# First two weight panels abreast and loaded in halves, a zeroed tile on TensorE before them, and other planner costs in the first block

## The chip, the cores and the metric

The kernel runs on one core of a Trainium2 chip. TensorE (PE; its weight loads are shown as PEld) multiplies, VectorE (DVE), ScalarE (ACT) and GpSimd (POOL) do the elementwise work, and SyncE (SP) issues all DMAs from one queue in order. The metric is the device time of one execution in microseconds; the profiled execution is one of them, looked at by the hardware profiler.

## The reference

Two transformer blocks follow one another on x of 512 tokens by 1024 features, all in float32. Of the first block the part that matters here is its beginning:

```
h = rmsnorm(x) * norm_mix_g
z = h @ w_in                      # 1024 x 5888: qa, ka, va, qb, kb, vb, ga, gb
y_a = mixer_a(qa, ka, va)         # 8 heads of full attention, 2 key/value heads, axial rope
y_b = mixer_b(qb, kb, vb)         # 3 groups of 4 heads, dilated bands, relative bias by bucket
x = x + (sigmoid(ga + b) * (y_a @ w_out_a) + sigmoid(gb + b) * (y_b @ w_out_b)) @ w_out
x = x + relu(rmsnorm(x) @ w_ff1)**2 @ w_ff2
x = x + sigmoid(rmsnorm(x) @ w_ple_gate) * (p @ w_ple)
```

A final norm and the second block follow: a SwiGLU layer, a mixer of retention and differential attention, attention to a memory, a second SwiGLU layer and the output norm.

## The kernel before, in words

Activations lie transposed, features on the 128 partitions and the 512 tokens along the row, so x is 8 tiles of 128x512 (256 KB each). Every float32 operand is split into a high part and a low part in a faster format, and a product is three matmuls: high by high, high weight by low activation, low weight by high activation. The weights come as panels: a panel is 8 blocks of 128x128 side by side (128x1024, 512 KB), it gives one 128x512 output tile, and it takes 8 x 3 = 24 matmuls, one triple per x tile. `take` (L456) makes a panel: one load from the packed weights, two ScalarE copies (`p.th`, tile `wh`, L467) that make the high part in halves of 512 columns, and two VectorE or four GpSimd subtractions (`p.tl`, tile `wl`, L469) that make the low part. Raw, high and low each have three buffers, so a panel's load waits for the low part of the panel three before.

Nothing is ordered by the hardware alone: `build` writes one list per engine, and each engine runs its list strictly in order, with semaphore waits. The lists come from a planner. Each helper (`v_tt`, `a_act`, `b_mm`, ...) appends an operation and moves the engine's planned clock by a cost formula; DMAs get a planned landing time from `dma_fin`. `flow` holds jobs (generators: a normalisation, a head's scores, a softmax, a split) and fills (panels). It steps the first job whose input is planned to be ready 0.15 us before TensorE's planned clock, and otherwise puts one more triple of a panel on TensorE. So the cost formulas decide after how many panel matmuls each step of a job is written into the lists, and `sooner` chooses VectorE or GpSimd by them.

A panel's parts are placed by `place_panels` at marks that the panels before it leave: the load on SP at the end of the panel five before (panels 0 to 4 at marks written out by hand, `first_load`), high and low parts one per step of the panel two before (panel 2's after the last step of panel 0, panels 0 and 1 after the rows of x tiles 0 and 3).

The beginning: SP loads the gain columns, x tile 0, panel 0, x tiles 1 to 4, panel 1, x tiles 5 to 7, a table `mats`, panel 2, three small tables (`relb`, `hot`, `mask`), panels 3 and 4, then `sel` and `rope` (about 0.5 MB each). `first_rows` makes h's high part (ScalarE) and low part (VectorE) of each x tile; `first_sum` squares the 8 tiles on ScalarE and adds them on VectorE for the norm's scale. `relative` makes the relative-bias table: three full-precision matmuls of `hot` and `relb`, an addition of `mask` on VectorE, a store to DRAM (`d_tab`, eight copies of each row), and twelve gathers from it into the bias tiles, which wait for the store. The panels come in the order qb, kb of group 0, 1 and 2 (panels 0 to 5), then vb, and so on. A head group's scores (`scores_b`) need the two projected tiles split, and two of the four PSUM banks that jobs use; those are released by VectorE's addition of the bias (tile `pB`).

Of the kernel before, what the change touches and what calls it, by code (L numbers as in the profile page):

```python
# [5 lines left out]
KT = DM // 128  # L6
# [18 lines left out]
NHOT = NX0 + 2 * NX1  # L25

# [66 lines left out]
def build(nc, d):  # L93
# [80 lines left out]
    def a_act(out, in_, func, *waits, **kw):  # L174
        cost = 0.1 + 0.00082 * size(in_) + 0.06 * ("bias" in kw) + 0.08 * ("accum_out" in kw)
        if "scale" in kw and not isinstance(kw["scale"], float):
            cost += 0.1
        return act.add(lambda e: e.activation(out, in_, func, **kw), cost, waits)  # L178

    def v_tt(out, a, b, op, *waits):  # L180
        return dve.add(lambda e: e.tensor_tensor(out, a, b, op), 0.065 + 0.00105 * size(a), waits)  # L181

    def v_stt(out, a, s, b, op0, op1, *waits, rev=False):
        return dve.add(lambda e: e.scalar_tensor_tensor(out, a, s, b, op0, op1, reverse0=rev), 0.1 + 0.00105 * size(a), waits)  # L184

    def v_ts(out, a, s1, s2, op0, op1, *waits):
        return dve.add(lambda e: e.tensor_scalar(out, a, s1, s2, op0, op1), 0.12 + 0.0006 * size(a), waits)

    def v_red(out, a, op, *waits, negate=False):
        return dve.add(lambda e: e.tensor_reduce(out, a, X, op, negate=negate), 0.065 + 0.00105 * size(a), waits)  # L190

    def v_cp(out, a, *waits):
        return dve.add(lambda e: e.tensor_copy(out, a), 0.065 + 0.00105 * size(a), waits)

    def v_ttr(out, a, b, scale, first, op0, op1, acc, *waits):
        return dve.add(lambda e: e.tensor_tensor_reduce(out, a, b, scale, first, op0, op1, acc), 0.08 + 0.00105 * size(a), waits)

    def v_rcp(out, a, *waits):
        return dve.add(lambda e: e.reciprocal(out, a), 0.07 + 0.0063 * size(a), waits)

    def p_tt(out, a, b, op, *waits):
        return pool.add(lambda e: e.tensor_tensor(out, a, b, op), 0.1 + 0.0022 * size(a), waits)  # L202
# [4 lines left out]
    def p_mul(out, a, s, *waits):  # L207
        return pool.add(lambda e: e.tensor_scalar(out, a, s, 1.0, ALU.mult, ALU.mult), 0.07 + 0.0012 * size(a), waits)
# [6 lines left out]
    def e_tt(out, a, b, op, *waits):  # L215
        n = size(a)
        return (v_tt if sooner(waits, 0.065 + 0.00105 * n, 0.2 + 0.0022 * n) else p_tt)(out, a, b, op, *waits)

    def e_mul(out, a, s, *waits):
        n = size(a)  # L220
        return (v_mul if sooner(waits, 0.12 + 0.0006 * n, 0.17 + 0.0012 * n) else p_mul)(out, a, s, *waits)

    table = [None]
# [64 lines left out]
    def b_mm(bank, out, lhsT, rhs, *waits):  # L288
        first, w = opened(bank)
        n = 0.0025 + size(rhs) / 2400  # L290
        n = max(n, 0.055) if lhsT.dtype == F32R else max(4 * n, 0.108)
        bank.done = pe.add(lambda e: e.matmul(out, lhsT, rhs, start=first, stop=True, skip_group_check=True), n, w, waits)  # L292
        return bank.done
# [143 lines left out]
    first_loads, first_parts = [], []  # L437
# [8 lines left out]
    def parts_here(after):  # L446

        low = (dve if not first_parts else pool) if len(panels) < 3 else panels[-1].low
        act.t = max(act.t, after) + 1.04
        low.t = max(low.t, act.t - 0.5) + (2.4 if low is pool else 1.2)  # L450

    def take(s):

        p = Panel()
        p.i, p.n = len(panels), len(s[3])
        i, width = p.i, s[2] * p.n  # L456
        p.width, p.off = width, panels[-1].off + 128 * panels[-1].width if panels else 0
        panels.append(p)
        order.append(s)
        src = d["wts"][p.off:p.off + 128 * width].rearrange("(p n) -> p n", p=128)  # L460
        raw, p.H, p.L = raw_t[i % 3], wh_t[i % 3], wl_t[i % 3]
        H, L = p.H, p.L
        behind = max(dve.t, pe.t) + 1.2 > max(pool.t, pe.t) + 2.4
        p.low = low = pool if (behind if i > 3 else i > 0) else dve
        p.cut = 256 if low is pool else 512
        p.load = Op(sp, lambda e: e.dma_start(raw[:, 0:width], src), [panels[i - 3].tl] if i >= 3 else [], raw_sem[i % 3])
        p.th = [Op(act, lambda e, c=c: e.activation(H[:, c], raw[:, c], FN.Copy), [p.load])  # L467
                for c in (slice(o, min(o + 512, width)) for o in range(0, width, 512))]
        p.tl = [Op(low, lambda e, c=c: e.tensor_tensor(L[:, c], raw[:, c], H[:, c].bitcast(F32), ALU.subtract),  # L469
                   [p.load, p.th[c.start // 512]]) for c in (slice(o, min(o + p.cut, width)) for o in range(0, width, p.cut))]  # L470
# [12 lines left out]
    def ran(p):  # L483

        p.steps.append(marks())
        if len(p.steps) == 3:
            parts_here(panels[p.i - 1].done.fin if p.i else 0.0)

    def place_panels():
        for p in panels:  # L490
            if p.i >= 3:
                assert panels[p.i - 3].done is not None
                p.th[0].waits.append(panels[p.i - 3].done)
            if p.i >= 5:
                panels[p.i - 5].steps[-1][sp].append(p.load)
            else:
                first_loads[p.i].append(p.load)
            for n, op in enumerate(p.th + p.tl):
                if p.i >= 2:
                    at_ = panels[p.i - 2].steps  # L500
                    at_[min(1 + n, len(at_) - 1) if p.i > 2 else -1][op.lane].append(op)
                else:
                    first_parts[p.i][op.lane].append(op)
# [18 lines left out]
    def panel(s, ops, ring, then, n=512, leave=None):  # L522
# [5 lines left out]
        spawn(then(b))  # L528

# [316 lines left out]
    def first_rows(k):  # L846
# [3 lines left out]
        if k in (0, 3):  # L850
# [25 lines left out]
    first_load()  # L876
    first_load()
# [11 lines left out]
    def relative():  # L889
# [10 lines left out]
        t_row = dma(tab_d, tab_t[:, :].unsqueeze(1).to_broadcast([4, COPIES, NHOT]), s_row, [tk for _, tk in parts])  # L900
        for g, wd in enumerate((256, 128, 128)):
# [16 lines left out]
    def proj_b(pr, g, i):  # L918
# [17 lines left out]
        return panel(feat("w_in", (QB, KB_)[i] + 128 * (2 * g + pr)), h1, FIL, then)  # L936
# [456 lines left out]
    for pr in range(2):  # L1393
        for g in range(3):
            for i in range(2):
                fills.append(proj_b(pr, g, i))
# [229 lines left out]

    RQ, RK, RV, RG, DQ, DK, DV = (512 * i for i in range(7))
    r, rcol = Rstd(21), Rstd()
    e = now()
# [793 lines left out]
```

How the kernel before makes its waits and increments, by code:

```python
            def go(eng):  # L2358
                for op in queues[ln]:
                    for key, value in op.emit:
                        eng.wait_ge(key.sem, value)
                    ins = op.fn(eng)
                    if isinstance(op.sem, DmaSem):
                        ins.then_inc(op.sem.sem, 16)
                    elif op.used:
                        ins.then_inc(ln.sem, 1)
                if ln is sp:
                    for o in outs:
                        eng.wait_ge(o.sem.sem, o.value)
```

## Time and profile before

| what | us |
|---|---|
| median of three runs (2056.57 to 2057.57) | 2057.19 |
| profiled execution | 2057.28 |
| its span, first to last instruction | 2055.4 |
| TensorE busy (9854 matmul records) | 2023.5 |
| VectorE / ScalarE / GpSimd busy | 1123.9 / 889.6 / 344.4 |
| mean granted TensorE clock | 0.995 |

Start times are counted from the span's first instruction. A row of the timeline gives the start, the duration, the engine, the line, the operation, what it writes and reads, how many were merged, and in brackets how long the engine was idle before and what ended that. A busy TensorE is not TensorE at its peak, since records of neighbouring matmuls overlap and a matmul at half clock is busy for longer. A granted clock of 1.00 is the 2.4 GHz level, 0.50 the 1.2 GHz level.

### The profile page before, as it was taken

The page shows a single profiled execution, that of the slowest core. Times are in us where ns is not written, and L with a number is a line of the kernel's source. Part 1 is how long each engine was busy: PE and PEld are TensorE (multiplying, and loading weights), DVE is VectorE, ACT ScalarE, POOL GpSimd, SP SyncE. Part 2 cuts the span into 40 slices and gives each one's busy share as a digit, 9 for nine tenths or more (in the row PEclk, how much of TensorE's full clock was granted, in tenths as well). Part 3 has the DMA queues.
Part 4 walks back from the last instruction along what each step waited for, and adds up shares of the span by engine and source line. Part 5 has one row for each costly group of instructions (what it writes and reads, how often), then busy time and mean ns, then how long its engine had stood idle before and what let it go on. Part 6 is the DMA issues. An engine that isn't in the chain of part 4 may idle for free.

```text
span 2055.4 us, 25244 instructions
## 1 busy us (share of the span) xinstructions
PE 2023.5 (98%) x9854; PEld 1684.2 (82%) x9854; DVE 1123.9 (55%) x1964; ACT 889.6 (43%) x1750; POOL 344.4 (17%) x337
## 2 busy tenths in 40 slices
PE   8999999999999999999999999999999999999997
PEld 6888778888888888878888888788898888888886
DVE  6767774455434344665443435787775664443434
ACT  5545553345423233553232325777655453322224
POOL 3224330021000001432110101232211021110102
PEclk9999999999999999999999999999999999999999
DMA  5221112243232322233323223223342033233322
GB/s 186 83 73 62 42 43 74 78 158 111 94 101 92 103 92 88 89 103 102 100 94 103 92 82 116 74 73 103 102 140 83 28 116 102 92 95 101 97 87 72
DMA packets 61635, 191.53 MB, mean 93 GB/s; under 512 B 6792, under 2 KB 14472, under 8 KB 61516
## 3 DMA queue, kind: packets, MB, share of 16 engines
q1 hardware_dynamic: 61516, 189.93, 28.7%
q8 instruction: 77, 1.26, 0.2%
q14 instruction: 42, 0.34, 0.1%
HBM read 187.69 MB, written 2.21 MB: 92 GB/s over the span
## 4 chain that ended last, share of the span: by engine, by line
PE 92%; DVE 5%; ACT 1%; DMA 1%; issue 1%; SPq 0%; DVEq 0%; ACTq 0%
PE bank L292 90%; PE bank L297 1%; DVE wl L469 1%; DVE work L190 1%; DVE tmp L181 0%; SPq L169 0%; ACT wh L467 0%; DMA raw<-d_wts 0%; DMA d_tab<-tab_sb 0%; ACT pB L178 0%; ACT rsq L178 0%; DVE x_sb L181 0%; DVE tmp L184 0%; DVE work L181 0%; DVE ssum L181 0%
## 5 line engine op out<-in xcount | busy, mean ns | idle before, releaser
L467 ACT ACTIVATE wh<-raw 128x512 fp32r<-128x512 f32 (+1 forms) x700 | 403.7, 610 | 891.4 <-PE bank L292 887.6
L292 PE MATMUL bank<-h_h,wh 128*128 128x512 f32 x1536 | 609.9, 397 | 7.3 <-ACT wh L467 6.1
L292 PE MATMUL bank<-h_l,wh 128*128 128x512 f32 x1536 | 600.6, 391 | 1.3 <-DVE h_l L184 1.2
L292 PE MATMUL bank<-h_h,wl 128*128 128x512 f32 x1536 | 600.1, 391 | 0.0
L469 DVE TENSOR_TENSOR wl<-raw,wh 128x512 fp32r<-128x512 f32 (+1 forms) x632 | 423.1, 695 | 60.9 <-ACT wh L467 38.8
L292 PEld LDWEIGHTS bank<-h_h,wh 128*128 128x128 f32 x1536 | 289.6, 189 | 71.1 <-ACT wh L467 6.1
L292 PEld LDWEIGHTS bank<-h_l,wh 128*128 128x128 f32 x1536 | 289.8, 189 | 63.5 <-DVE h_l L184 3.7
L292 PEld LDWEIGHTS bank<-h_h,wl 128*128 128x128 f32 x1536 | 289.5, 188 | 61.0 <-DVE wl L469 0.3
L469 POOL TENSOR_TENSOR wl<-raw,wh 128x256 fp32r<-128x256 f32 x134 | 107.1, 826 | 350.5 <-ACT wh L467 350.5
L202 POOL TENSOR_TENSOR tmp<-tmp,rstd 128x512 f32<-128x512 f32 x44 | 63.4, 1442 | 469.4 <-ACT tmp L178 469.4
L181 DVE TENSOR_TENSOR tmp<-bank,rstd 128x512 f32<-128x512 f32 x98 | 70.4, 721 | 115.1 <-PE bank L292 114.5
L181 DVE TENSOR_TENSOR x_sb<-x_sb,bank 128x512 f32<-128x512 f32 x56 | 38.5, 687 | 141.2 <-PE bank L292 141.2
L181 DVE TENSOR_TENSOR tmp<-tmp,bank 128x512 f32<-128x512 f32 x53 | 36.4, 687 | 139.3 <-PE bank L292 133.1
L184 DVE SCALAR_TENSOR_TENSOR x_sb<-bank,x_sb 128x512 f32<-128x512 f32 (+1 forms) x51 | 33.6, 660 | 123.5 <-PE bank L292 123.5
L292 PE MATMUL bank<-f1act_h,wh 128*128 128x512 f32 x256 | 99.6, 389 | 0.0
L292 PE MATMUL bank<-f1act_l,wh 128*128 128x512 f32 x256 | 99.6, 389 | 0.0
L292 PE MATMUL bank<-f1act_h,wl 128*128 128x512 f32 x256 | 99.6, 389 | 0.0
L202 POOL TENSOR_TENSOR ssum<-ssum,tmp 128x512 f32<-128x512 f32 (+1 forms) x52 | 70.6, 1362 | 134.4 <-ACT tmp L178 133.3
L202 POOL TENSOR_TENSOR ssum<-tmp,tmp 128x512 f32<-128x512 f32 (+1 forms) x9 | 12.4, 1385 | 472.9 <-ACT tmp L178 472.9
L292 PE MATMUL bank<-f3act_h,wh 128*128 128x512 f32 (+1 forms) x194 | 71.8, 370 | 0.0
L292 PE MATMUL bank<-f3act_h,wl 128*128 128x512 f32 (+1 forms) x194 | 71.7, 369 | 0.0
L292 PE MATMUL bank<-f3act_l,wh 128*128 128x512 f32 (+1 forms) x194 | 71.6, 369 | 0.0
(476 smaller groups left out, 3317.0 us busy)
## 6 DMA issues: line engine op xcount, KB each, us to landing
raw<-d_wts SPq DMA_DIRECT2D x314, 512.0 KB, 3.5
raw<-d_wts SPq DMA_DIRECT2D x24, 384.0 KB, 3.0
x_sb<-d_xT SPq DMA_DIRECT2D x16, 256.0 KB, 5.5
raw<-d_wts SPq DMA_DIRECT2D x24, 128.0 KB, 2.0
d_yT<-x_sb SPq DMA_DIRECT2D x4, 384.0 KB, 2.9
tab<-d_ali SPq DMA_DIRECT2D x4, 256.0 KB, 4.3
tab<-d_dec SPq DMA_DIRECT2D x4, 256.0 KB, 3.8
mraw<-d_memT SPq DMA_DIRECT2D x8, 128.0 KB, 2.4
```

The source lines that it names most:

```text
L181: return dve.add(lambda e: e.tensor_tensor(out, a, b, op), 0.065 + 0.00105 * size(a), waits)
L184: return dve.add(lambda e: e.scalar_tensor_tensor(out, a, s, b, op0, op1, reverse0=rev), 0.1 + 0.00105 * size(a), waits)
L190: return dve.add(lambda e: e.tensor_reduce(out, a, X, op, negate=negate), 0.065 + 0.00105 * size(a), waits)
L202: return pool.add(lambda e: e.tensor_tensor(out, a, b, op), 0.1 + 0.0022 * size(a), waits)
L292: bank.done = pe.add(lambda e: e.matmul(out, lhsT, rhs, start=first, stop=True, skip_group_check=True), n, w, waits)
L297: bank.done = pe.add(lambda e: e.transpose(out, in_, ident), 0.11, w, waits)
L467: p.th = [Op(act, lambda e, c=c: e.activation(H[:, c], raw[:, c], FN.Copy), [p.load]) for c in (slice(o, min(o + 512, width)) for o in ran ...
L469: p.tl = [Op(low, lambda e, c=c: e.tensor_tensor(L[:, c], raw[:, c], H[:, c].bitcast(F32), ALU.subtract), [p.load, p.th[c.start // 512]]) ...
```

## The change

It has five parts. At the start VectorE zeroes a 128x128 piece of a scratch tile and TensorE multiplies it by itself nine times in full precision; ScalarE's table for exponentials is loaded there too. The columns go behind x tile 0, and panels 0 and 1 are loaded in halves of 512 columns, in turn with x tiles 1 to 3; both get their low parts on VectorE, one half after each of the rows 0 to 3. Panels 0 and 1 run abreast: for each x tile three matmuls of the one, then three of the other. Panel 5's load moves ahead of `sel` and `rope`, the job `relative` yields between its store and the gathers (so the gathers are written when the planner's clock has passed the store's landing), and panels 2 and 3 have their parts placed at other steps. Until the second block's mixer (`late`) the planner uses other, mostly larger costs, and `ran` books the cost of a panel's parts step by step.

```
+    zero = T.slots[-1].ap[:, 0:128]
+    t_zero = dve.add(lambda e: e.memset(zero, 0.0), 0.2)
+    b = ALL.get()
+    for _ in range(WARM):                                  # WARM = 9
+        b_mm(b, b.ap[:, 0:128], zero, zero, t_zero)
+    b.free = [b.done]
+    T.slots[-1].free = [b.done]
+    act_table(EXP)
+    load_x([0])
     t_cols = dma(cols_t[:, :], d["cols"], DmaSem("s_cols"))
-    def first_load():
+    def first_load(kb=512):
         first_loads.append(sp.mark())
-        return dma_fin(512 * 1024, 0.0)
-    load_x([0])
-    w_fin = [first_load()]
-    load_x([1, 2, 3, 4])
-    w_fin.append(first_load())
-    load_x([5, 6, 7])
+        return dma_fin(kb * 1024, 0.0)
+    w_fin = []
+    for k in range(4):
+        if k:
+            load_x([k])
+        w_fin.append(first_load(256))
+    load_x([4, 5, 6, 7])
...
-        if k in (0, 3):
+        if k < 4:
             parts_here(w_fin[len(first_parts)])
             first_parts.append(marks())
...
-    first_load()
-    first_load()
+    for _ in range(3):
+        first_load()
     t_sel = dma(sel_t[:, :], d["sel"], DmaSem("s_sel"))
...
         t_row = dma(tab_d, tab_t[:, :].unsqueeze(1).to_broadcast([4, COPIES, NHOT]), s_row, [tk for _, tk in parts])
+        yield [t_row]
...
+        if i < 2:
+            p.loads = [Op(sp, lambda e, c=c: e.dma_start(raw[:, c], src[:, c]), [], raw_sem[i] if c.start else DmaSem(f"s_raw{i}a"))
+                       for c in (slice(0, 512), slice(512, width))]
...
-            if p.i >= 5:
-                panels[p.i - 5].steps[-1][sp].append(p.load)
+            if p.i >= 6:
+                panels[p.i - 5].steps[-1][sp].extend(p.loads)
...
-                    at_[min(1 + n, len(at_) - 1) if p.i > 2 else -1][op.lane].append(op)
+                    at_[min(n + (1 if p.i > 3 else 7 if p.i == 2 else KT), len(at_) - 1)][op.lane].append(op)
...
+    def abreast(items, ops, ring):
+        if not ring.idle(len(items))():
+            yield ring.idle(len(items))
+        bs, ps = [ring.get() for _ in items], [take(s) for s, _ in items]
+        for k, t in enumerate(ops):
+            if t.rdy is None:
+                yield have(t)
+            for b, p in zip(bs, ps):
+                ...
+                b_mm(b, out, wH, t.h, high(p, k), t.rdy[0])
+                b_mm(b, out, wH, t.l, t.rdy[1])
+                p.done = b_mm(b, out, wL, t.h, low(p, k))
+                ran(p)
+                yield
```

The costs, in us for a row of n elements (left before, right until `late` is set):

```
ScalarE  activation       0.1   + 0.00082 n     0.19 + 0.00085 n   (accumulator +0.08 / +0.19)
VectorE  tensor_tensor    0.065 + 0.00105 n     0.14 + 0.00108 n
VectorE  scalar_tensor_t. 0.1   + 0.00105 n     0.16 + 0.00108 n
VectorE  tensor_scalar    0.12  + 0.0006 n      0.22 + 0.00053 n
GpSimd   tensor_tensor    0.1   + 0.0022 n      0.15 + 0.00235 n
TensorE  split formats    max(0.0025 + n/2400, 0.055)     max(0.013 + n/2400, 0.111 or 0.06)
```

## Rows read from the trace of the kernel before

**Rows 1.** Table by stretch: busy us (instructions) per engine, granted clock, DMA share, GB/s.
```profile
0.00:6.14 6.14, 0.00 (x1) 0.00 (x1) 0.75 (x1) 2.69 (x4) 0.20 (x4) 1.00 0.61 194
6.14:18.31 12.17, 11.11 (x30) 6.51 (x30) 9.23 (x12) 10.15 (x19) 3.72 (x4) 1.00 0.92 319
24.12:58.83 34.71, 32.85 (x178) 26.43 (x176) 22.62 (x44) 19.86 (x53) 11.22 (x15) 1.00 0.39 126
...
200.00:320.00 120.00, 112.45 (x537) 91.55 (x537) 90.16 (x176) 63.46 (x143) 43.21 (x45) 0.96 0.13 42
320.00:880.00 560.00, 560.00 (x2480) 463.79 (x2479) 265.17 (x404) 218.18 (x376) 57.39 (x53) 1.00 0.31 100
```

**Rows 2.** List of waits, TensorE, 200 to 330 us: total, times, longest.
```profile
PE bank L297 <- DVE pa L187: 3.7, 1, 3.7
```

**Rows 3.** Timeline of TensorE, first 25 us.
```profile
6.14 0.79 PE L292 MATMUL bank<-h_h,wh 128*128 128x512 f32 x1 [6.14 <-ACT wh L467]
...
18.31 1.67 PE L292 MATMUL bank<-hot_sb,relb_sb 32*4 32x383 f32 x6
...
24.12 0.39 PE L292 MATMUL bank<-rsqr,m1024r 128*128 128x512 f32 x1
```

**Rows 4.** DMA view, 0 to 60 us in 40 slices of 1.5 us.
```profile
GB/s 0 106 360 300 332 412 396 414 416 266 133 156 410 413 77 0 85 284 33 35 0 116 147 130 154 137 245 401 391 38 0 0 0 0 191 377 134 8 0 0
```

**Rows 5.** Timeline of VectorE and ScalarE, 13 to 21 us.
```profile
13.03 3.19 DVE L184 SCALAR_TENSOR_TENSOR h_l<-x_sb,cols_sb,h_h 128x512 fp32r<-128x512 f32 x3 [1.59 <-ACT h_h L178]
14.43 0.31 ACT L178 ACTIVATE m1024r<-mats_sb 128x128 fp32r<-128x128 f32 x1 [0.28 <-DMA mats_sb<-d_mats]
14.65 4.26 ACT L178 ACTIVATE tmp<-x_sb 128x512 f32<-128x512 f32 x8
18.82 2.18 ACT L467 ACTIVATE wh<-raw 128x512 fp32r<-128x512 f32 x4
```

**Rows 6.** Timeline of SP's DMA issues, 16 to 38 us.
```profile
16.09 0.43 SPq L169 DMA_DIRECT2D sel_sb<-d_sel  x1
16.56 0.43 SPq L169 DMA_DIRECT2D rope_sb<-d_rope  x1
23.62 0.33 SPq L466 DMA_DIRECT2D raw<-d_wts  x1
23.99 0.77 SPq L169 DMA_DIRECT2D d_tab<-tab_sb  x1
30.48 7.30 SPq L169 DMA_DIRECT2D bias<-d_tab  x12
```

**Rows 7.** Chain of waits in order of time: start, us, what.
```profile
23.99 6.47 DMA d_tab<-tab_sb
```

**Rows 8.** Timeline of VectorE at the first bias additions.
```profile
40.46 0.69 DVE L181 TENSOR_TENSOR pB<-bank,bias 128x512 f32<-128x512 f32 x1 [3.96 <-DMA bias<-d_tab]
41.79 0.68 DVE L181 TENSOR_TENSOR pB<-bank,bias 128x512 f32<-128x512 f32 x1
```

**Rows 9.** Timeline of TensorE: first scores' first and last row, second scores' two waits.
```profile
35.55 0.39 PE L292 MATMUL bank<-qb001h,qb000h 64*128 64x256 f32 x2
...
37.08 0.28 PE L292 MATMUL bank<-qb001l,qb000h 64*128 64x192 f32 x2
47.69 0.33 PE L292 MATMUL bank<-qb011h,qb010h 64*128 64x128 f32 x2 [0.59 <-ACT qb011h L178]
48.76 0.33 PE L292 MATMUL bank<-qb011l,qb010h 64*128 64x128 f32 x2 [0.63 <-DVE qb011l L181]
```

**Rows 10.** Table by stretch, TensorE alone: busy us (records), granted clock, DMA share, GB/s.
```profile
220.03:223.44 3.41, 3.41 (x11) 0.50 0.07 26
281.47:284.88 3.41, 2.28 (x16) 1.00 0.51 156
284.88:291.70 6.82, 5.40 (x15) 0.50 0.00 0
```

**Rows 11.** Groups of instructions on VectorE, 0 to 320 us: busy us, mean ns.
```profile
L181 DVE TENSOR_TENSOR tmp<-bank,rstd 128x512 f32<-128x512 f32 x22 | 18.3, 830 | 2.8 <-PE bank L292 2.8
```

More of the change, by code:

```diff
@@ L192, in v_cp @@
     def v_cp(out, a, *waits):
[L193 removed]
+        return dve.add(lambda e: e.tensor_copy(out, a), (0.065 + 0.00105 * size(a) if late else 0.14 + 0.00108 * size(a)), waits)
     def v_ttr(out, a, b, scale, first, op0, op1, acc, *waits):
[L196 removed]
+        return dve.add(lambda e: e.tensor_tensor_reduce(out, a, b, scale, first, op0, op1, acc), (0.08 + 0.00105 * size(a) if late else 0.22 + 0.00108 * size(a)), waits)
@@ L207, in p_mul @@
     def p_mul(out, a, s, *waits):
-        return pool.add(lambda e: e.tensor_scalar(out, a, s, 1.0, ALU.mult, ALU.mult), 0.07 + 0.0012 * size(a), waits)
+        return pool.add(lambda e: e.tensor_scalar(out, a, s, 1.0, ALU.mult, ALU.mult), (0.07 + 0.0012 * size(a) if late else 0.17 + 0.0016 * size(a)), waits)
     def sooner(waits, dve_cost, pool_cost):
@@ L446, in parts_here @@
     def parts_here(after):
-        low = (dve if not first_parts else pool) if len(panels) < 3 else panels[-1].low
-        act.t = max(act.t, after) + 1.04
-        low.t = max(low.t, act.t - 0.5) + (2.4 if low is pool else 1.2)
+        act.t = max(act.t, after) + 0.61
+        dve.t = max(dve.t, act.t) + 0.69
     def take(s):
@@ L462, in take @@
         H, L = p.H, p.L
-        behind = max(dve.t, pe.t) + 1.2 > max(pool.t, pe.t) + 2.4
-        p.low = low = pool if (behind if i > 3 else i > 0) else dve
+        if late and i not in lows:
+            lows[i] = pool if max(dve.t, pe.t) + 1.2 > max(pool.t, pe.t) + 2.4 else dve
+        p.low = low = lows.pop(i) if i in lows else pool if i > 1 else dve
         p.cut = 256 if low is pool else 512
-        p.load = Op(sp, lambda e: e.dma_start(raw[:, 0:width], src), [panels[i - 3].tl] if i >= 3 else [], raw_sem[i % 3])
-        p.th = [Op(act, lambda e, c=c: e.activation(H[:, c], raw[:, c], FN.Copy), [p.load])
+        if i < 2:
+            p.loads = [Op(sp, lambda e, c=c: e.dma_start(raw[:, c], src[:, c]), [], raw_sem[i] if c.start else DmaSem(f"s_raw{i}a"))
+                       for c in (slice(0, 512), slice(512, width))]
+        else:
+            p.loads = [Op(sp, lambda e: e.dma_start(raw[:, 0:width], src), [panels[i - 3].tl] if i >= 3 else [], raw_sem[i % 3])]
+        p.th = [Op(act, lambda e, c=c: e.activation(H[:, c], raw[:, c], FN.Copy), [p.loads[c.start // 512 if i < 2 else 0]])
                 for c in (slice(o, min(o + 512, width)) for o in range(0, width, 512))]
         p.tl = [Op(low, lambda e, c=c: e.tensor_tensor(L[:, c], raw[:, c], H[:, c].bitcast(F32), ALU.subtract),
-                   [p.load, p.th[c.start // 512]]) for c in (slice(o, min(o + p.cut, width)) for o in range(0, width, p.cut))]
+                   [p.th[c.start // 512].waits[0], p.th[c.start // 512]])
+                for c in (slice(o, min(o + p.cut, width)) for o in range(0, width, p.cut))]
         p.done, p.steps = None, [marks()]
@@ L485, in ran @@
         p.steps.append(marks())
-        if len(p.steps) == 3:
-            parts_here(panels[p.i - 1].done.fin if p.i else 0.0)
+        if late and len(p.steps) == 3:
+            act.t = max(act.t, panels[p.i - 1].done.fin) + 1.04
+            panels[-1].low.t = max(panels[-1].low.t, act.t - 0.5) + (2.4 if panels[-1].low is pool else 1.2)
+        if late:
+            return
+        n, i = len(p.steps) - 2, p.i + 2
+        if n == 0 and not late:
+            behind = max(dve.t, pe.t) + 1.39 > max(pool.t, pe.t) + 3.2
+            lows[i] = pool if (behind if i > 3 else i > 1) else dve
+        if n < 2:
+            act.t = max(act.t, panels[p.i - 1].done.fin + 0.13 if p.i else 0.0) + 0.61
+            th_fin[i, n] = act.t
+        elif i in lows or panels[-1].i >= i:
+            low = lows[i] if i in lows else panels[i].low
+            if low is dve and n < 4:
+                dve.t = max(dve.t, th_fin[i, n - 2] + 0.13) + 0.69
+            elif low is pool and n < 6:
+                pool.t = max(pool.t, th_fin[i, (n - 2) // 2] + 0.13) + 0.8
     def place_panels():
@@ L935, in then @@
             t.free = yield from split(qk[pr][g][i], t.ap[:, :], tk)
-        return panel(feat("w_in", (QB, KB_)[i] + 128 * (2 * g + pr)), h1, FIL, then)
+        return feat("w_in", (QB, KB_)[i] + 128 * (2 * g + pr)), then
     def proj_vb(g, pr):
@@ L1394, in build @@
         for g in range(3):
-            for i in range(2):
-                fills.append(proj_b(pr, g, i))
+            both = [proj_b(pr, g, i) for i in range(2)]
+            if pr == g == 0:
+                fills.append(abreast(both, h1, FIL))
+            else:
+                fills.extend(panel(s, h1, FIL, then) for s, then in both)
         fills.extend(proj_vb(g, pr) for g in (1, 2, 0))
@@ L1623, in build @@
     sm = sm_next[0]
+    late.append(True)
     RQ, RK, RV, RG, DQ, DK, DV = (512 * i for i in range(7))
```

45 lines of the change are left out of this document (30 added, 15 removed).

## The prediction

> **What bounds the kernel now.** I read the table of stages first, because the share of busy time (98% on TensorE) is an average over very different stretches. From 320 to 880 us TensorE is busy all 560 us at a granted clock of 1.00: the change reorders work there at most, and there is nothing to win [rows 1]. What the first block loses lies in four places of the same table: 6.14 us before the first matmul, then 12.17 us that hold only 30 records, 1.86 us idle between 24 and 59 us, and 7.55 us idle between 200 and 320 us, where the mean clock is 0.96. The list of waits gives the largest single piece of the last: 3.7 us for a normalised softmax block on VectorE [rows 2]. Then I followed the chain of waits from the other end. Up to 59 us it does not run over TensorE but over the relative-bias table: the table's store to DRAM takes 6.47 us [rows 7], the twelve gathers are then issued one by one until 37.78 [rows 6], and VectorE waits for the last until 40.46 [rows 8]. So the start of this kernel has two limits side by side, the loads of x and the bias table, and a gain on one counts only as far as the other lets it.
>
> **The start (half loads, two panels abreast, zeroed tile).** Today the first matmul waits for panel 0's high part, which waits for all of its 512 KB; 30 matmuls are done at 18.31, then the bias table's own matmuls take 1.67, and the other 18 of the first two panels end at 24.12: (24.12 - 19.98) / 18 = 0.23 us each [rows 3]. In the new queue x tile 0, the columns and half a panel are ahead of the first matmul, 256 KB less; at the 300 to 416 GB/s of the first slices [rows 4] that is 0.6 to 0.9 us, so it starts at about 5.4. What stands ahead of the last x tile is the same 3 MB in both orders. Its low part ends today at 13.03 + 3.19 = 16.22 [rows 5]; the new order puts panel 1's two low parts on VectorE between the tiles (some 1.4 us more) and takes GpSimd's four away from beside them, and I leave it at 16.3. With two panels abreast each tile feeds 6 matmuls instead of 3, so 5 tiles, again 30 matmuls, can be done at about 15.4.
>
> Then comes a point that the diff does not touch. The planner emits the bias-table matmuls when its TensorE clock has passed the due time of the three small tables (13.6 us by its own DMA sum, with the same bytes ahead as before). By its new sums TensorE passes that after tile 4 of both panels: after the 30th matmul, as today. On the chip mats land at 14.43 [rows 5]; 512 KB of panel 2 and 127 KB of tables follow, 639 KB at 0.4 MB per us = 1.6, an estimate of 16.0; at 18.31 they were there, as no wait for them is shown. Between the two I take 16.4, near the estimate. Then 16.4 + 1.7 + 18 x 0.23 = 22.2, against 24.12: 1.9 us won. Bounds: 2.9 with the tables already there (15.4 instead of 16.4), 0 if they land at 18.3. The memset, the nine zero matmuls and the early table load lie before any x tile is there and cost nothing; if the zero tile ended late, it would push the first matmul by as much, at most 1 us.
>
> The Trainium skill, "TensorE: Matmul & The Clock Gate", section "HAM oscillation — how this bites in real kernels", says that short bursts between DMA waits lose the full clock again each time; by it the zero tile's clock is gone when the half-busy stretch after it ends, and 30 matmuls take 30 x 0.46 = 13.8 us.
>
> **The SP queue.** This is the part that I think costs. Today sel and rope leave at 16.09 and 16.56, into idle DMA time; panel 5's load waits for panel 2's low parts until 23.62, and the table's store leaves behind it at 23.99 [rows 6]. The diff moves panel 5's load ahead of sel and rope, so both now wait for panel 2's low parts too, and the store behind all three. Panel 2's high parts still stand behind the eight squares on ScalarE (14.65 to 18.9, then 18.82 [rows 5]), so panel 5 leaves near 23.6 again, sel and rope 0.47 each after it, and the store at 24.7. It finds 1.03 MB more in the rings: at 0.41 MB per us 2.5 us. So it lands at 30.48 + 0.7 + 2.5 = 33.7 instead of 30.48. The twelve gathers take 37.78 - 30.48 = 7.3 to issue as before, and the last bias lands at 33.7 + (40.46 - 30.48) = 43.7 instead of 40.46 [rows 6, 8]: 3.2 us late, bounds 0.7 (the store passes the big transfers) and 5 (panel 2's low parts a little later as well). The Trainium skill, "DMA: Bandwidth & Descriptors", section "Queues, rings and completion order", says that each DMA engine takes its descriptors in ring order: by that the 2.5 us stand; no row here shows a small transfer behind big ones. In return the new wait before the gathers lets panel 6's load leave ahead of them and not behind.
>
> **What that does to TensorE.** The first scores run at 35.55; the second pair waits at 47.69 and 48.76 for a split that stands behind the exponentials [rows 9]. Following the new costs through the planner, the first scores come after 7 of panel 4's 8 tiles and the second after 2 of panel 5's, so 24 x 3 + 6 = 78 panel matmuls after panel 1, where today there are (47.69 - 0.59 - 24.12 - 0.5 - 1.8) / 0.23 = 90. TensorE is there at 22.2 + 78 x 0.23 + 0.5 (two mean matmuls) + 1.8 (first scores, 35.55 to 37.36 [rows 9]) = 42.4. It needs both banks, which VectorE empties 2.0 us after the bias lands (40.46 to 41.79 + 0.68 [rows 8]): 45.7. So it waits 3.3 us where it waited 1.2. Made comparable by the 12 matmuls that are now still to do, 2.8 us, it stands at 48.5 against 48.76: the 1.9 us are spent but for 0.3. The bounds at this place: +2.1 (bias only 0.7 late, the start's gain kept), and -3.5 (bias 5 us late, and the wait takes the clock down). That a wait can do so is in the table: TensorE busy 2.28 of 3.41 us, then 6.82 us at a granted clock of 0.50, the 1.2 GHz level [rows 10].
>
> **The measured costs.** What they touch is 200 to 320 us: 7.55 us idle [rows 1], and 3.41 + 5.40 us of busy time at half clock [rows 10], of which half is lost, 4.4: together 12.0. There the planner steps a softmax, a transpose or a split when it thinks its input is ready. Today it puts 0.60 us on a 128x512 VectorE operation and 0.216 on a matmul, 2.8 matmuls long; the rows show a mean of 0.83 for such an operation [rows 11] and 0.23 for a matmul, 3.6. The new costs say 0.69 and 0.226, 3.1: a third of the error. So a step is put behind more panel matmuls, and waits shrink; they do not all go, because the low part of a panel ahead in VectorE's queue is still placed by the panel's steps. A later head costs nothing at its end, since panels without any wait follow from 320 on [rows 1]. I take half, 6.0; bounds 12.0 and -3.0 (a reshuffled order with one more wait like that of rows 2, less some).
>
> **Sum.** 0.3 + 6.0 = 6.3 us off the profiled execution's 2057.28 (its span of 2055.4 and 1.9 around it; the median of the three runs is 2057.19): 2051.0.
>
> **Rivals.**
> Slower: the bias table takes over. If the gathers land after about 44, TensorE stands before the second scores for 5.5 us or more and comes out of it at half clock: 5.5 + 3.4/2 = 7.2, and another 1.7 us of half clock and blocked splits before the third scores; less the 1.9 of the start and the 1.2 of waits that were there, +5.8, with the stretch from 200 on as it is: 2063. For it: the chain already runs here, and three transfers more stand before the store. Against it: panel 6 is no longer behind the gathers.
> No change: the start is eaten as above and the waits from 200 on move to other heads: 2057. For it: the order of panels and their low parts is the same there, and costs moved by a tenth reshuffle rather than mend.
> Everything works: the store leaves early enough that the bias lands as today, so 1.9 and the waits of 1.2 are kept as gain, and all 12.0 go: 2042. Against it: VectorE is still busy 90 of 120 us in that stretch [rows 1].
> The zeroed tile does not do what it says: the 30 matmuls run at half the pace, 5.4 + 13.8 = 19.2 instead of 16.4 before the tables. That is 2.8 us, and the wait of 3.3 before the second scores hides all of it: 2051, inside the forecast.
>
> **Numbers.** Forecast 0.46 (its own range 2046 to 2055), no change 0.23, slower 0.16, everything 0.15. A change under 0.2%, 4.1 us, cannot be told from none. Faster: 0.39 of the forecast and 0.15 = 0.54; the same: 0.07 + 0.22 + 0.01 = 0.30; slower: 0.15 + 0.01 = 0.16. The range leaves out about half of each outer case: 2043 to 2061.
>
> **What would show it.** In the new profile: the first matmul of a panel near 5.4; the table matmuls near 16.4 after 30 panel matmuls, with a short wait before them; the first two panels done near 22.2; sel, rope and the store behind panel 5's load after 23; the bias near 43.7 and a wait of 3 us or so before the second scores; from 200 to 320 about half the idle time and half the time at the lower clock. I am wrong if the store leaves with nothing ahead of it, if the second scores come at another place, or if the idle time from 200 on stays.

## The result and the profile after

The changed kernel takes 2042.4 us (median of 2041.69 to 2043.28), the kernel before beside it 2056.88 (2056.29 to 2057.57): a ratio of 0.993, 95% interval 0.9912 to 0.9947. The profiled execution is 2041.82, its span 2040.0 where it was 2055.4, and the mean granted clock 0.998 where it was 0.995.

The table by stretch of the changed kernel, in the stretches of [rows 1]:

```profile
6.14:18.31 12.17, 11.48 (x35) 7.63 (x36) 9.60 (x15) 10.71 (x20) 0.00 (x0) 1.00 0.96 337
24.12:58.83 34.71, 34.02 (x186) 27.64 (x184) 26.29 (x44) 19.02 (x54) 14.21 (x15) 1.00 0.51 162
200.00:320.00 120.00, 119.30 (x598) 99.26 (x597) 100.39 (x194) 68.87 (x152) 45.06 (x44) 1.00 0.17 53
320.00:880.00 560.00, 558.69 (x2465) 462.07 (x2463) 277.21 (x415) 220.06 (x378) 42.86 (x29) 1.00 0.32 101
```

From 200 to 320 us TensorE is idle for 0.70 us instead of 7.55, the clock is 1.00 instead of 0.96, and 598 matmul records stand where 537 stood. The list of waits of its TensorE, 0 to 330 us, has nothing left of [rows 2] (its 3.7 us wait for VectorE's softmax block):

```profile
PE bank L301 <- ACT wh L480: 1.2, 1, 1.2
PE bank L301 <- DVE tmp L875: 1.1, 1, 1.1
PE bank L301 <- DVE pB L182: 0.6, 1, 0.6
PE bank L301 <- DMA mask_sb<-d_mask: 0.3, 1, 0.3
PE bank L301 <- ACT pa L179: 0.3, 1, 0.3
PE bank L301 <- DVE outa_l L182: 0.3, 1, 0.3
```

TensorE's timeline at the start and at the second scores, which answers to [rows 3, 9]:

```profile
1.05 4.21 PE L301 MATMUL bank<-tmp 128*128 128x128 f32 x18 [1.05 <-DVE tmp L875]
6.47 0.79 PE L301 MATMUL bank<-h_h,wh 128*128 128x512 f32 x1 [1.21 <-ACT wh L480]
17.18 1.67 PE L301 MATMUL bank<-hot_sb,relb_sb 32*4 32x383 f32 x6 [0.32 <-DMA mask_sb<-d_mask]
22.99 0.39 PE L301 MATMUL bank<-h_h,wh 128*128 128x512 f32 x1
39.18 0.39 PE L301 MATMUL bank<-qb001h,qb000h 64*128 64x256 f32 x2
44.28 0.32 PE L301 MATMUL bank<-qb011h,qb010h 64*128 64x128 f32 x1 [0.59 <-DVE pB L182]
```

SP's DMA issues, for [rows 6]:

```profile
11.87 11.71 SPq L479 DMA_DIRECT2D raw<-d_wts  x3
23.62 0.43 SPq L170 DMA_DIRECT2D sel_sb<-d_sel  x1
24.10 0.43 SPq L170 DMA_DIRECT2D rope_sb<-d_rope  x1
24.58 0.77 SPq L170 DMA_DIRECT2D d_tab<-tab_sb  x1
26.66 3.85 SPq L479 DMA_DIRECT2D raw<-d_wts  x2
31.84 7.36 SPq L170 DMA_DIRECT2D bias<-d_tab  x12
```

VectorE's first bias addition, for [rows 8]:

```profile
42.22 0.69 DVE L182 TENSOR_TENSOR pB<-bank,bias 128x512 f32<-128x512 f32 x1 [1.89 <-DMA bias<-d_tab]
```

To see where the time went I count, for each stretch, what TensorE **loses**: the stretch's length less the matmuls it starts there, each at the distance to the next that its shape usually has at full clock (0.227 us for 128x512). Waits and half clock are both in it. All these kernels hold the same work by this count, the zeroed tile left out. It is an estimate: another choice of the usual distance shifts whole columns by 1 or 2 us; the differences between rows from 200 to 330 us change by a few tenths. The medians are of all executions of a kernel, the losses of one profiled execution. Two executions, one of e14 (9146 us) and one of the kernel before beside e14, e15 and e10 (6688 us), are over three times as long as the rest and are left out of the ratios.

| kernel | median, us | before beside it | 0-24.2 | 24.2-60.2 | 60.2-200 | 200-330 | 330-1200 |
|---|---|---|---|---|---|---|---|
| before | 2056.88 | | 11.6 | 7.0 | 8.2 | 14.5 | 2.2 |
| after | 2042.4 | 2056.88 | 10.5 | 5.5 | 7.9 | 2.3 | 2.0 |
| e13 no new start | 2042.0 | 2055.87 | 10.5 | 5.1 | 7.9 | 2.3 | 1.9 |
| e7 no zeroed tile | 2042.01 | 2056.09 | 10.2 | 5.8 | 7.7 | 2.3 | 1.9 |
| e5 panel 5 last | 2041.88 | 2055.87 | 10.5 | 4.6 | 7.9 | 2.1 | 2.2 |
| e6 no yield | 2051.55 | 2056.09 | 11.6 | 12.9 | 9.4 | 2.4 | 2.0 |
| e15 yield alone | 2056.02 | 2056.1 | 10.2 | 7.6 | 8.2 | 12.5 | 2.2 |
| e1 costs alone | 2049.19 | 2056.09 | 10.7 | 9.2 | 9.2 | 3.0 | 5.0 |
| e4 engine costs alone | 2048.97 | 2055.49 | 10.2 | 5.1 | 8.5 | 6.3 | 4.1 |
| e3 TensorE cost alone | 2058.21 | 2055.49 | 11.4 | 10.6 | 11.6 | 10.4 | 0.6 |
| e8 booking alone | 2052.8 | 2055.49 | 11.1 | 9.9 | 10.6 | 5.3 | 2.2 |
| e2 start, booking, yield; old costs | 2051.07 | 2056.09 | 9.3 | 9.8 | 9.1 | 5.3 | 2.2 |
| e14 costs and booking | 2047.31 | 2056.1 | 10.5 | 6.0 | 7.9 | 2.6 | 1.9 |
| e9 before, VectorE costs x 1.02 | 2055.62 | 2055.49 | 10.5 | 7.6 | 7.9 | 13.0 | 3.3 |
| e10 before, x 0.98 | 2058.97 | 2056.1 | 11.1 | 6.4 | 8.4 | 13.9 | 4.9 |
| e11 after, x 1.02 | 2048.14 | 2055.87 | 9.3 | 6.9 | 8.7 | 4.1 | 4.7 |
| e12 after, x 0.98 | 2044.2 | 2055.87 | 10.2 | 5.3 | 7.9 | 4.4 | 2.0 |

Of the 15.3 us between before and after in this table, 12.2 come from 200 to 330 us, 1.5 from 24 to 60 and 1.1 from the start.

### The profile page after: what moved, and what is told of

It reads as the page before. It is cut to its first block, busy times and chain, and to the rows that moved or that the text cites. A ratio compares the mean times of both kernels' runs of the same rounds, so it can differ in the third digit from the quotient of the medians.

```text
span 2040.0 us, 25256 instructions
## 1 busy us (share of the span) xinstructions
PE 2021.1 (99%) x9872; PEld 1686.5 (83%) x9872; DVE 1142.2 (56%) x1992; ACT 887.6 (44%) x1749; POOL 316.5 (16%) x288
## 4 chain that ended last, share of the span: by engine, by line
PE 94%; DVE 3%; ACT 1%; DMA 1%; SPq 1%; issue 0%; POOL 0%; DVEq 0%; ACTq 0%
PE bank L301 93%; PE bank L306 1%; SPq L170 0%; DMA d_tab<-tab_sb 0%; DMA x_sb<-d_xT 0%; ACT tmp L179 0%; ACT rsq L179 0%; DVE x_sb L182 0%; DVE wl L482 0%; DVE tmp L185 0%; DVE work L191 0%; ACT wh L480 0%; DVE pd L185 0%; POOL wl L482 0%; ACT h_h L179 0%
## 5 line engine op out<-in xcount | busy, mean ns | idle before, releaser
L482 DVE TENSOR_TENSOR wl<-raw,wh 128x512 fp32r<-128x512 f32 (+1 forms) x654 | 442.4, 703 | 69.2 <-ACT wh L480 47.6
L482 POOL TENSOR_TENSOR wl<-raw,wh 128x256 fp32r<-128x256 f32 x90 | 74.9, 859 | 269.4 <-ACT wh L480 269.3
```

## The experiments

The first two were argued between theory C (the gain comes from the new costs) and theory S (it comes from the new start, and the other order that follows it). Later M is closer costs and booking, O any other order, A that the parts add up, D and G that 24 to 60 us falls well only by the new start or by a good draw, and Y and R are two readings of the yield.

**The new costs alone, and everything without them.** e1 is before with the new cost formulas; e2 is after with the old ones.

```
e1:  -  cost = 0.1 + 0.00082 * size(in_) + ...
     +  cost = (0.1 + 0.00082 * size(in_) ... if late else 0.19 + 0.00085 * size(in_) ...)
     ...                                   # the other formulas of the change, nothing else
e2:  the same lines, the other way round, in the changed kernel
```

> The kernel before with the new cost formulas alone, up to the second block's mixer; start, queue and the booking of panel parts as before. Theory C (the formulas put each step behind more panel matmuls, whatever the start): the 7.6 us of idle time and the 10.2 us at half clock between 200 and 330 us go, the start stays at 24.1 for the first two panels, 2045 (2043 to 2048). Theory S (the other start and the new booking shift the order, and the waits fall away by that): 2052 to 2060, with waits of 2 us and more left in that stretch.

> The changed kernel with the old cost formulas: halves, abreast, zeroed tile, queue order, and the new booking of panel parts stay. Theory C: the first two panels end near 23.0 as in the changed kernel, the waits between 200 and 330 us are back with some 12 us, 2054 (2051 to 2058). Theory S: no wait over 0.6 us there, 2042 to 2046.

Measured: 2049.19 (ratio 0.9968, 0.9955 to 0.9982) and 2051.07 (0.9974, 0.9963 to 0.9985). Neither theory has it: each half alone wins 5 to 7 us. The costs alone clear 200 to 330 (3.0 lost), but without them the stretch is better too (5.3). Both lose 9 to 10 us between 24 and 60 us, where before lost 7. So two things act on 200 to 330, and something else on 24 to 60.

**The yield.** e6 is after without it.

```
         t_row = dma(tab_d, ...)
-        yield [t_row]
```

> The changed kernel without the wait of the planner between the bias table's store and its gathers, so the gathers stand directly behind the store on SP and panel 6's and 7's loads behind them. If the yield carries the 1.4 us won between 24 and 60 us: panel 6 lands 8 us later, near 41 to 42, and the stretch loses 1 to 4 us, 2044 to 2046. If it carries nothing (bias lands near 42 either way, panel 6 is needed near 42): 2042.4 within 0.7.

Measured: 2051.55 (0.9978, 0.9969 to 0.9988), so that line is worth 9.2 us here, far over what I had put down. The timeline of its ScalarE, then of its TensorE:

```profile
43.62 0.63 ACT L480 ACTIVATE wh<-raw 128x512 fp32r<-128x512 f32 x1 [12.14 <-DMA raw<-d_wts]
45.20 0.61 ACT L179 ACTIVATE qb001h<-tmp 128x512 fp32r<-128x512 f32 x1
```

```profile
45.87 0.58 PE L301 MATMUL bank<-qb001h,qb000h 64*128 64x256 f32 x2 [5.43 <-ACT qb001h L179]
```

Without the yield the next panels' loads are issued only behind the twelve gathers, at 38.77 instead of 26.66 and after. ScalarE, in order, then stands 12.14 us at a panel's high part, and the splits for the scores stand behind it; TensorE waits 5.43 us for one and 1.64 for the next, and is at half clock from 43 to 53 us. It is neither the bias table nor the gathers that are late, it is a panel's load.

**The zeroed tile.** e7 is after without the nine matmuls.

```
-    for _ in range(WARM):
-        b_mm(b, b.ap[:, 0:128], zero, zero, t_zero)
```

> The changed kernel without the nine matmuls of the zeroed tile. In the changed kernel the first panel matmuls ran at 0.43 us start to start until 12.6 all the same, at the half-clock pace. If the zeroed tile does nothing: the table matmuls wait for their landing at 17.2 as before and the time is 2042.4 within 0.7. If it does what it says: 0.5 to 2 us slower, the granted clock rising later than 13.0.

Measured: 2042.01 (0.9932, 0.9915 to 0.9948), the time of the changed kernel. Its first panel matmul is at 6.49 (6.47 with the tile), and in both the first 13 or 14 matmuls stand 0.43 us apart or more, nearly twice the 0.227 of full clock, before they go on at 0.23 from 13.0 on (the kernel before does so from 11.9 on). The clock column shows 1.00 for all of that, as in [rows 1], but the trace of the changed kernel has its first record of the clock at 13.02 us: ahead of it only the distances tell the level. The tile itself ran at half pace as well: its 18 records of 128 columns stand 0.21 us apart, 1.67 ns a column, where the six full-precision records of 383 columns at 17.18 take 0.84. They end at 5.26, and the tile changes nothing that comes after. So the tile buys nothing, as in the rival that the prediction put beside the Trainium skill ("TensorE: Matmul & The Clock Gate", "HAM oscillation — how this bites in real kernels"), but not in that way: no full clock was lost again, none had been reached, and some 14 of the 30 matmuls ran at half pace, not all 30.

**What of the costs, and the booking.** Four kernels built on before: VectorE's costs times 1.02 (e9), the new TensorE cost alone (e3), the other new costs alone (e4), the new booking of panel parts alone (e8).

```
e9:  -  self.t = op.fin = max(self.t, ready(op.waits)) + cost
     +  self.t = op.fin = max(self.t, ready(op.waits)) + cost * (1.02 if self.name == "vector" and not late else 1.0)
e3:  -  n = 0.0025 + size(rhs) / 2400
     +  n = max(n + 0.013, load)           # and the other forms of b_mm
e4:  the formulas of e1 but this one
e8:  -  if len(p.steps) == 3:
     -      parts_here(panels[p.i - 1].done.fin if p.i else 0.0)
     +  n, i = len(p.steps) - 2, p.i + 2
     +  ...                                # all that `ran` and `take` have new
```

> The kernel before, with every planned VectorE cost of the first block times 1.02 and nothing else: a shake, 0.014 us on a 128x512 operation, which mends no estimate (0.60 becomes 0.615, the rows of before show a mean of 0.83). Theory O (the old order between 200 and 330 us is an unlucky one; any other order loses less): the 14.5 us that TensorE loses there fall under 8, and the time is 2045 to 2052. Theory M (closer costs are what clears the waits there): 10 us or more are still lost there, 2054 to 2059.

> The kernel before with the new TensorE cost alone (0.226 us a matmul for 0.216, and 0.111 for small ones). Theory M in the form that the matmul's cost matters (steps are placed by TensorE's clock): the loss of 14.5 us between 200 and 330 us falls under 6, 2046 to 2051. In the form that the engines' costs matter: it makes the operations look still shorter against a matmul, 2.66 matmuls long instead of 2.78 where the rows say 3.6, so the waits stay or grow, 2057 to 2062. Theory O: under 8 lost there, sign of the cost no matter.

> The kernel before with the new costs of VectorE, ScalarE and GpSimd alone (0.69 us for a 128x512 VectorE operation, 3.2 of its matmuls where it was 2.78). Theory M in the form that the engines' costs matter: it does as all the new costs together did, about 3 us lost between 200 and 330 us where it was 14.5, 2046 to 2050, perhaps better. In the form that the matmul's cost matters: 10 or more lost, 2055 to 2058. Theory O: under 8 lost there, 2045 to 2053.

> The kernel before with the new booking of a panel's parts alone (each part is booked at the step where it stands, with the choice of VectorE or GpSimd made there; panel 1's low parts go to VectorE), at the old costs and with the old start. The new start at the old costs, which has this booking, lost 5.3 us between 200 and 330 us where before lost 14.5. If the booking did that: 4 to 7 lost there, 2046 to 2052. If it was the other order after a new start: 10 or more lost, 2054 to 2058. Theory O says under 8 lost, as for any other order.

Measured: e9 2055.62 (1.0003, 0.9993 to 1.0012), e3 2058.21 (1.001, 1.0001 to 1.002), e4 2048.97 (0.9969, 0.9957 to 0.998), e8 2052.8 (0.9987, 0.9978 to 0.9997). The stretch from 200 to 320 in the table of TensorE, first e9, then e4, then e8:

```profile
200.00:320.00 120.00, 113.06 (x549) 0.97 0.14 44
```

```profile
200.00:320.00 120.00, 115.88 (x568) 1.00 0.18 54
```

```profile
200.00:320.00 120.00, 117.97 (x589) 1.00 0.15 49
```

A shake moves little (113.06 busy where 112.45 was; 13.0 lost in e9, 13.9 in e10 below), so theory O falls. The engine costs alone take the loss from 14.5 to 6.3, the booking alone to 5.3, the TensorE cost alone to 10.4: three parts that each clear a piece. Both kinds of cost together reach 3.0 (e1), and with the booking 2.3 to 2.6; only e5 goes a little below, to 2.1. The booking and the TensorE cost pay for it between 24 and 200 us (20.5 and 22.2 lost where it was 15.2), so that e8 missed the time that I expected, 2046 to 2052, and e3 the loss under 6 of theory M's form for the matmul's cost.

"Closer" in theory M is not shown. On VectorE two 128x512 operations in a row start 0.60 us apart (296.74 and 297.34 in before, each recorded as 0.68), so the old cost of 0.60 was its pace already where nothing disturbs it. What e4 shows is that longer planned costs of the other engines help.

How the old order waits is seen in before itself at 280 us, on VectorE, then on TensorE:

```profile
279.38 1.37 DVE L469 TENSOR_TENSOR wl<-raw,wh 128x512 fp32r<-128x512 f32 x1 [1.99 <-ACT wh L467]
280.67 0.68 DVE L190 TENSOR_REDUCE work<-bank 128x1 f32<-128x512 f32 x1
281.65 0.88 DVE L187 TENSOR_SCALAR pa<-pa,work 128x512 f32<-128x512 f32 x2
```

```profile
282.50 1.05 PE L292 MATMUL bank<-mats_sb,tmp 128*128 128x1 f32 x8 [0.97 <-ACT pa L178]
287.38 0.79 PE L292 MATMUL bank<-ka_h,qa1h 128*128 128x512 f32 x1 [1.42 <-DVE pta_l L181]
```

VectorE stands 1.99 us at a panel's low part, whose high part is late on ScalarE; the softmax behind it comes too late for TensorE, which waits 0.97 us, drops to half clock at 284.88 [rows 10], and there waits again. In the changed kernel's list of waits for VectorE no low part waits for a high part between 200 and 330 us (3.2 us in before).

The booking alone does not take that wait away. In e8 low parts wait for 4.4 us there, and the same wait stands at the same place, on VectorE, while TensorE goes on:

```profile
278.12 0.69 DVE L471 TENSOR_TENSOR wl<-raw,wh 128x512 fp32r<-128x512 f32 x1 [1.99 <-ACT wh L469]
```

```profile
281.55 0.95 PE L293 MATMUL bank<-mats_sb,tmp 128*128 128x1 f32 x8
285.73 0.50 PE L293 MATMUL bank<-ka_h,qa1h 128*128 128x512 f32 x1 [0.23 <-DVE pta_l L181]
```

What differs is TensorE's list: ahead of the row at 281.55 it has 15 panel matmuls in a row where before had 12, and between the next two transposes of the softmax block (`pa`) 9 where before had 3. So the steps stand behind more panel matmuls, and the wait on VectorE is covered. The old planner booked a panel's parts once, after its third step; the new `ran` books each where it stands, and it also books more for them (VectorE's two low parts 1.38 us for 1.2, GpSimd's four 3.2 for 2.4). Which of the two moved the steps is not shown.

With the costs alone (e1) the wait does go: no low part on VectorE waits for a high part. But there the planner also gives more low parts to GpSimd, since VectorE looks later to it. The groups of low parts on GpSimd from 200 to 330 us, before and e1 (four instructions a panel):

```profile
L469 POOL TENSOR_TENSOR wl<-raw,wh 128x256 fp32r<-128x256 f32 x20 | 15.3, 781 | 10.1 <-ACT wh L467 10.1
L477 POOL TENSOR_TENSOR wl<-raw,wh 128x256 fp32r<-128x256 f32 x44 | 34.6, 814 | 53.5 <-ACT wh L475 53.5
```

VectorE is left with 4 low-part instructions where it had 12. No run holds that choice fixed, so how much of the gain of the costs is the steps' place and how much is GpSimd's help stays open. It is not what the booking works by: e8 has 20 on GpSimd, as before.

**Without the new start; the order of SP; two shakes of the changed kernel.** e13 is before with costs, booking and yield. e5 is after with panel 5's load behind `sel` and `rope`. e11 and e12 are after with the factor of e9.

```
e13: none of  WARM, halves in p.loads, abreast, load_x/first_load in turn, "for _ in range(3)"
e5:  -    for _ in range(3):
     -        first_load()
     +    first_load()
     +    first_load()
          t_sel = dma(...)
          t_rope = dma(...)
     +    first_load()
e11: cost * (1.02 if self.name == "vector" and not late else 1.0);   e12: 0.98
```

> The kernel before with all new costs, the new booking of a panel's parts and the wait ahead of the gathers, but with the old start (whole panels, one after the other, no zeroed tile, panel 5's load behind sel and rope). Theory A (the parts add up: costs and booking clear 200 to 330 us, the yield keeps the second scores from the bias table, the start is worth what its own stretch shows, 1.1 us): about 11.6 us lost until 24.2, 5 to 7 until 60.2, 2 to 4 between 200 and 330, time 2043 to 2046. Theory D (the new start is needed for the second scores to fall well): the stretch from 24 to 60 us loses 9 or more, as in each part alone, and the time is 2047 to 2051.

> The changed kernel with panel 5's load put back behind sel and rope, which then leave near 16 us as before, so that the table's store has only panel 5 ahead of it. By the prediction's step the two transfers ahead of the store cost 2.5 us: the store would land 2.5 us sooner than its 31.83 and the last bias near 39.7. By the trace of the changed kernel, where the store took 7.25 us and 6.47 before, 0.8 us: bias near 41.4. By both TensorE waits for nothing at the second scores any more (0.6 us now), and the time falls by 0.6 at most: 2041.5 to 2042.5. If sel and rope are in the way of panels 3 and 4 it rises, to 2043 or more.

> The changed kernel with every planned VectorE cost of the first block times 1.02. Theory A (closer costs and booking give an order that keeps its distance from the waits): 2 to 5 us lost between 200 and 330 us, 5 to 7 between 24 and 60, time 2041 to 2045. Theory G (the changed kernel's order is a good draw at the second scores, where four of the partial versions lost 9 to 10 us): 9 or more lost between 24 and 60, 2046 to 2050.

> The same with the factor 0.98, so the other way: theory A 2041 to 2045, with 2 to 5 us lost between 200 and 330 us and 5 to 7 between 24 and 60; theory G 9 or more lost between 24 and 60 in this one or in the one with 1.02, 2046 to 2050.

Measured: e13 2042.0 (0.9932, 0.9918 to 0.9945), e5 2041.88 (0.9929, 0.9916 to 0.9941), e11 2048.14 (0.9962, 0.9949 to 0.9976), e12 2044.2 (0.9943, 0.9929 to 0.9956). e13 went below what I expected of it (2043 to 2046): without half loads, abreast panels and zeroed tile the kernel is as fast. Its TensorE at the start, and that of e15 (below), which has the old start and the old costs:

```profile
6.75 0.80 PE L300 MATMUL bank<-h_h,wh 128*128 128x512 f32 x1 [6.75 <-ACT wh L476]
15.73 1.67 PE L300 MATMUL bank<-hot_sb,relb_sb 32*4 32x383 f32 x6
22.95 0.39 PE L300 MATMUL bank<-rsqr,m1024r 128*128 128x512 f32 x1
```

```profile
16.87 1.67 PE L292 MATMUL bank<-hot_sb,relb_sb 32*4 32x383 f32 x6
22.67 0.39 PE L292 MATMUL bank<-rsqr,m1024r 128*128 128x512 f32 x1
```

The first two panels end at 22.95 and 22.67 with the old start, at 22.99 with the new one. The 24.12 of [rows 3] is a late execution of the same order: ten profiles with the old start lose 10.2 to 11.6 us until 24.2, seven with the new one 9.3 to 11.6. So the 1.1 us of the start are not shown to be the change's. e5 and e13, with and without the new start and both with panel 5's load last, take 2041.88 and 2042.0.

In e5 the store is issued at 23.52 and the gathers behind it at 30.06, 6.54 us later, where after has 24.58 and 31.84, 7.26. The first bias addition runs at 40.80 instead of 42.22, and the time is the same: TensorE waited only 0.59 us there.

The shakes: 200 to 330 us keeps most of its gain (4.1 and 4.4 lost), as theory A said, and neither loses 9 us between 24 and 60 as theory G wanted. But e11's time is outside A's range, as it lost more elsewhere: a 0.93 us wait for VectorE's bias addition at 42.99 with half clock until 47.5 behind it, and 4.7 us after 330. So some 6 us of the changed kernel's time hang on its exact order.

**The yield again, and the other shake.** e15 is before with the yield alone, e14 is e13 without it, e10 is before with the factor 0.98.

> The kernel before with the wait ahead of the gathers and nothing else. In it ScalarE's split for the second scores stood behind a panel's high part until 47.03, and that panel's load behind the gathers until 37.83; TensorE waited twice, 1.2 us. Theory Y (the yield lets panel 6's load go ahead of the gathers, so that this split is no longer late): the load leaves near 27, the split is done before 40, 1 to 2 us less are lost between 24 and 60 us (5 to 6 where it was 7.0), 13 to 15 stay lost between 200 and 330, time 2053 to 2056. Rival R (the gathers, issued later, make the bias table the limit): the last bias lands later than 41.5 and TensorE waits for it 2 us or more, time 2057 to 2061.

> The kernel with costs and booking but with neither the new start nor the wait ahead of the gathers: one line less than the one that lost 5.07 us between 24 and 60 us and ran in 2042.0. Theory Y: the loads of panels 6 and 7 leave behind the gathers, at 36.5 or later, the splits for the scores stand behind their high parts, TensorE waits 3 us or more for ScalarE and comes out at half clock: 9 to 13 us lost there, time 2046 to 2050. Otherwise (the yield matters only with two panels abreast): 5 to 7 lost there, 2042 to 2044.

> The kernel before with every planned VectorE cost of the first block times 0.98. Theory M (closer costs and booking clear 200 to 330 us; this one is a little further off): 12 to 16 us lost there, 2055 to 2059. Theory O (the old order is a bad draw): under 8 lost there, 2046 to 2052.

Measured: e15 2056.02 (0.9999, 0.9989 to 1.0008), e14 2047.31 (0.9957, 0.9941 to 0.9973), e10 2058.97 (1.0017, 1.0007 to 1.0026). In e15 panel 6's load does leave early, at 25.09, but the list of ScalarE has the split still behind the exponentials, which run until 44.6, and behind high parts of a later panel:

```profile
44.54 1.13 ACT L467 ACTIVATE wh<-raw 128x512 fp32r<-128x512 f32 x2
45.58 0.61 ACT L178 ACTIVATE qb011h<-tmp 128x512 fp32r<-128x512 f32 x1
```

So theory Y falls in that form, and R too: the bias table came earlier than in before (39.01). The yield alone gives nothing. With the new start it gives 9.2 us (e6 to after). With costs and booking it gives 5.3 by the medians (e14 to e13), but e14 has two kinds of executions: the profiled one took 2042.38, three others 2046.65 to 2047.78, at a mean clock of 0.996 for 0.998. In the profiled one ScalarE again waits for a panel behind the gathers (7.37 us), the split ends at 44.0, and TensorE waits 0.44 and 0.95 us and stays at full clock: 6.0 us lost between 24 and 60, which is not the 9 to 13 of theory Y. That the other three lost the clock behind this wait is a guess, since their traces were not taken.

## Why the prediction was wrong

Forecast were 2051.0 us, between 2043 and 2061; it is 2042.4. The sign was right, the size too small.

- **What bounds the kernel, and 320 to 880 us:** right. Nothing was won there, and 200 to 320 was where most lay.
- **The measured costs, "I take half, 6.0":** the step that failed. From 200 to 330 us 12.2 us went, about the upper bound, and the costs alone (e1) take 11.5. That steps are put behind more panel matmuls was the right mechanism, and it shows at 280 us; the halving was wrong. Its reason was that the waits would not all go "because the low part of a panel ahead in VectorE's queue is still placed by the panel's steps". In e1, with the low parts placed as before, they go: the planner gives most low parts to GpSimd, and none on VectorE waits. In e8 the low part does stand in VectorE's queue and waits its 1.99 us, and TensorE waits only 0.23 behind it. The new booking in `ran` and `take`, which I had described and not priced, takes 9.2 of the 14.5 us lost there by itself; the two do not add up, they reach the same floor. The 0.83 us that the prediction read for a VectorE operation is the mean of the one group of [rows 11]; the three largest groups of that width have 0.69 to 0.75, and in a row such operations can start 0.60 apart, so "a third of the error" rests on one group.
- **The start, 1.9:** 1.1 between the two profiles, and nothing by e13 and e15. The 30 matmuls before the tables were right; the first one came at 6.47 and not 5.4, behind the half panel's high part, the tables at 17.18 and not 16.4. The zeroed tile does nothing by e7, as one rival had it, but without that rival's 2.8 us: the other 16 matmuls or so ran at full pace and were done before the tables landed.
- **The SP queue, 2.5 us for a store behind big transfers:** the order came as said (23.62, 24.10, 24.58), the size did not: the store took 7.25 us instead of the 6.47 of [rows 7]. The prediction named the Trainium skill's ring order for the 2.5 ("DMA: Bandwidth & Descriptors", "Queues, rings and completion order"); the trace agrees with that order, as sel and rope land near 28.0 and 29.4 (4.4 and 5.3 us after their issue) and the store near 31.8, but the price was 0.8. The store takes some 6.5 us without them, and most of their time lies inside that. The last bias was used from 42.22 on, 1.8 us late, where the forecast was 3.2 with a lower bound of 0.7.
- **The second scores, a wait of 3.3:** 0.59. Their place was right (after 7 tiles of panel 4, and 2 of panel 5). The table was 1.5 us earlier than forecast and TensorE 1.0 us later (43.37 for 42.4). What I passed over in half a sentence, panel 6's load leaving ahead of the gathers, is what keeps this place clear: without it 7.4 us more are lost (e6).
- **The rival "everything works", 2042,** has the time and its main term, all 12.0. Its condition did not hold: the bias was used 1.8 us later than before, and with only 0.59 us of wait behind it that did not matter. The prediction gave it 0.15.

The 2 to 3 us more that e1, e4, e10 and e11 lose after 330 us stand at one place: between 883 and 894 us TensorE waits 2.2 to 3.0 us for ScalarE's high part of h (`h_h`), where before and after wait 1.0 and 0.9, and in e1, e10 and e11 3.4 us at half clock follow. Still open: why that wait is longer in these orders, what the slower executions of e14 do, and the two questions left at 280 us.

## What to carry to other kernels

In a kernel whose lists a planner writes, price the bookkeeping of the planner like an operation: here it took 9.2 us of a loss of 14.5 by itself, and longer planned costs took 11.5. A wait on one engine is no loss by itself: ask whether the next engine has other work written ahead of what is waited for, as the same 1.99 us on VectorE cost TensorE a drop to half clock in one order and 0.23 us in another. When a transfer moves in an in-order queue, follow what stands behind it down to the next engine's queue; here a panel load behind twelve gathers stopped the splits for the scores. And before a gain is put down to a part, compare the stretch in more than one execution of the old kernel: 1.1 us at the start was spread between executions.

## What was not expected of the hardware

Waits of under 1 us can be followed by half clock, and need not be: in e11 TensorE was idle 0.40 and 0.93 us around 42 and ran at the 1.2 GHz level from 44.1 to 47.5 (granted clock 0.50), while the profiled execution of e14, with 0.44 and 0.95 at the same scores, stayed at 1.00, as did after with one wait of 0.59. And a store of 112 KB that had three transfers of 512 KB ahead of it was only 0.7 us later to land than with one ahead (7.26 us from its issue to that of the gathers, against 6.54 in e5).
